# Layer norms behind projections: shift by the mean of the first four tiles, squares of three pairs folded beside the last two projections

## What is computed

```python
def layer_norm_2(x, g, b):
    mu = jnp.mean(xf, -1, keepdims=True)
    var = jnp.mean(jnp.square(xf - mu), -1, keepdims=True)
    return ((xf - mu) * lax.rsqrt(var + LN_EPS_2) * g + b).astype(x.dtype)
...
    h = layer_norm_2(DEEPNORM_ALPHA * h + m, ln_g[i, 0], ln_b[i, 0])
```

## Time and profile before

| | us |
|---|---|
| median of 3 runs | 3078.92 |
| lowest, highest | 3077.69, 3083.2 |
| the profiled execution | 3076.58 |
| its span, first to last instruction | 3074.8 |
| TensorE matmuls busy | 2885.7 (94%) |
| VectorE busy | 858.7 (28%) |
| ScalarE busy | 348.2 (11%) |
| mean granted TensorE clock | 0.994 |

### The profile page before, as it was taken

The page is one execution under the profiler, slowest core; times in us unless marked ns, Lnnn a source line. Parts: engine busy times, 40 slices in busy tenths (PEclk is TensorE's granted clock), DMA queues, the critical chain, the costliest instruction groups (busy, mean ns, idle before and its releaser), DMA issues.

```text
span 3074.8 us, 39592 instructions
## 1 busy us (share of the span) xinstructions
PE 2885.7 (94%) x16504; PEld 2035.2 (66%) x16504; DVE 858.7 (28%) x1787; ACT 348.2 (11%) x710; POOL 52.8 (2%) x92
## 2 busy tenths in 40 slices
PE   6999999998888899999988888999999999999998
PEld 3554444476666667788644444588788887887887
DVE  1332321242222233331311111288522202222201
ACT  0022220020000011220100000101211001011000
POOL 1000000000000001000000000000000000000000
PEclk9999999999999999999999999999999999999999
DMA  8443335169999984234699999943333443342440
GB/s 328 166 156 128 127 119 214 69 243 420 421 417 421 420 349 137 86 102 148 235 421 421 420 420 421 374 147 124 107 123 110 151 151 110 123 144 89 156 144 36
DMA packets 97804, 684.05 MB, mean 222 GB/s; under 512 B 11632, under 2 KB 12784, under 8 KB 17136
## 3 DMA queue, kind: packets, MB, share of 16 engines
q1 hardware_dynamic: 91632, 660.17, 54.3%
q0 software_dynamic: 6016, 21.50, 2.3%
HBM read 678.22 MB, written 3.41 MB: 222 GB/s over the span
## 4 chain that ended last, share of the span: by engine, by line
PE 74%; DMA 22%; DVE 2%; ACT 1%; issue 1%; SPq 0%; ACTq 0%; DVEq 0%
PE ps L612 29%; DMA ring<-units 22%; PE ps L878 11%; PE ps L1044 6%; PE ps L907 3%; PE ps L1348 2%; PE ps L1183 2%; PE ps L630 2%; PE ps L621 1%; PE ps L703 1%; PE ps L699 1%; PE ps L1000 1%; PE ps L928 1%; PE ps L792 1%; PE ps L813 1%; PE ps L1030 1%
## 5 line engine op out<-in xcount | busy, mean ns | idle before, releaser
L612 PE MATMUL ps<-h,ring 128*128 128x256 f32 (+1 forms) x2176 | 501.3, 392 | 4.9 <-ACT h L1507 4.9
L612 PEld LDWEIGHTS ps<-h,ring 128*128 128x128 f32 x2176 | 411.8, 190 | 92.2 <-issue 37.8
L1059 PE MATMUL ps<-ring,arena 128*32 128x256 f32 x3072 | 380.7, 382 | 55.8 <-DMA ring<-units 52.0
L1044 PE MATMUL ps<-ring,arena 128*64 128x256 f32 x3072 | 352.0, 385 | 57.4 <-DMA ring<-units 53.3
L1044 PEld LDWEIGHTS ps<-ring,arena 128*64 128x64 f32 x3072 | 236.5, 138 | 165.7 <-issue 81.9
L1059 PEld LDWEIGHTS ps<-ring,arena 128*32 128x32 f32 x3072 | 184.2, 109 | 244.1 <-DMA ring<-units 102.7
L878 PE MATMUL ps<-u,ring 128*128 128x512 f32 (+1 forms) x1024 | 339.2, 487 | 0.0
L612 PE MATMUL ps<-arena,ring 128*128 128x256 f32 x1408 | 306.6, 379 | 4.7 <-DVE arena L2299 3.4
L612 PEld LDWEIGHTS ps<-arena,ring 128*128 128x128 f32 x1408 | 267.3, 190 | 42.1 <-DVE arena L2299 4.2
L878 PEld LDWEIGHTS ps<-u,ring 128*128 128x128 f32 x1024 | 193.6, 190 | 133.1 <-issue 119.6
L2213 DVE COPY u<-ps 32x512 f32<-32x512 f32 (+1 forms) x128 | 70.9, 554 | 212.4 <-PE ps L1059 119.9
(11 more groups left out here) (330 smaller groups left out, 2592.6 us busy)
## 6 DMA issues: line engine op xcount, KB each, us to landing
ring<-units SPq DMA_DIRECT2D x624, 1024.0 KB, 13.4
arena<-quarters POOLq DMA_DIRECT2D x32, 256.0 KB, 2.9
h<-tokens SPq DMA_DIRECT2D x1, 2048.0 KB, 24.6
arena<-neighbours POOLq DMA_DIRECT2D x32, 64.0 KB, 5.7
arena<-tokens POOLq DMA_DIRECT2D x1, 2048.0 KB, 9.0
arena<-memory POOLq DMA_DIRECT2D x2, 1024.0 KB, 6.3
con<-constants SPq DMA_DIRECT2D x1, 1712.0 KB, 23.1
early_values<-arena POOLq DMA_DIRECT2D x6, 256.0 KB, 5.0
```

The lines of the kernel that those rows point to most:

```text
L612: last = nc.tensor.matmul(ps[:, g + j, 0:n], w[:, kt, j * P:(j + 1) * P], rhs[:, q * KT + kt, 0:n], start=(q == 0 and kt == 0), stop=(q == ...
L1044: last = nc.tensor.matmul(ps[j * slots:(j + 1) * slots, bank, lo:lo + UC], lhsT[:, kt, 0:slots], w[j][:, kt, :], start=(kt == 0), stop=(kt ...
L1059: last = nc.tensor.matmul(ps[j % 4 * slots:(j % 4 + 1) * slots, banks[j // 4], 0:UC], lhsT[:, kt, 0:slots], w[j][:, kt, :], start=(kt == 0 ...
```

## The change

The mean is no longer formed as a whole before squaring. VectorE adds the first two residual pairs to one tile (tiles 0 to 3 folded), and TensorE multiplies this tile with the mean matrix in the middle of the third product (`middle`, `shift_sum`). Twice that value is the shift `off`. VectorE subtracts it from pairs 0 and 1, and for pairs 2 and 3 from the residual operand ahead of the products (`less_shift`). ScalarE squares pairs 0, 1 and 2 as they are ready. VectorE folds tiles 4 and 5 to `rest`, and the six square tiles to one. Behind the fourth product TensorE multiplies `rest`, the folded squares, tiles 6 and 7 and their squares: six matmuls. The variance is the mean square less the square of the rest of the mean, one VectorE instruction, with the square of the rest by ScalarE. VectorE subtracts the rest of the mean from each pair behind that, between the multiplies. In `layer`, `shift_and_values` moves behind the norm's matmuls, and the wait for `memory_loaded` ahead of them.

```diff
...
-            def project(rhs, n, tiles=2, groups=1, arrived=None):
+            def project(rhs, n, tiles=2, groups=1, arrived=None, middle=None):
...
+                        if middle and q == groups // 2 and j == 0:
+                            middle()
...
+            def shift_sum(folded, n, g):
+                pe.wait_ge(part_folded, at(part_folded))
+                nc.tensor.matmul(ps[:, g, 0:n], mean, folded[:, 0, 0:n], start=True, stop=True).then_inc(shift_summed, 1)
+
+            def rest_and_squares(x, sq, rest, n, g):
+
+                pe.wait_ge(rest_folded, at(rest_folded))
+                nc.tensor.matmul(ps[:, g, 0:n], mean, rest[:, 0:n], start=True, stop=False)
+                pe.wait_ge(squares_folded, at(squares_folded))
+                nc.tensor.matmul(ps[:, g + 1, 0:n], mean, sq[:, 0, 0:n], start=True, stop=False)
+                pe.wait_ge(centred, at(centred, KT // 2))
+                for kt in (KT - 2, KT - 1):
+                    last = nc.tensor.matmul(ps[:, g, 0:n], mean, x[:, kt, 0:n], start=False, stop=(kt == KT - 1))
+                last.then_inc(shift_left, 1)
+                pe.wait_ge(squares_ready, at(squares_ready, KT // 2))
+                for kt in (KT - 2, KT - 1):
+                    last = nc.tensor.matmul(ps[:, g + 1, 0:n], mean, sq[:, kt, 0:n], start=False, stop=(kt == KT - 1))
+                last.then_inc(squares_summed, 1)
...
+            def project_and_normalize(rhs, x, sq, n, folded, rest, groups=1, after=None, arrived=None, between=None):
+
+                g = 2 * (state["product"] % 4)
                 for c in range(KT // 2):
-                    project(rhs, n, groups=groups, arrived=None if c else arrived)
-                    if c:
-                        sums(x, n, c - 1, g, *((products_taken, first + c) if taken
-                                               else (residual_ready, at(residual_ready))))
-                sums(x, n, KT // 2 - 1, g, *((products_taken, first + KT // 2) if taken
-                                             else (residual_ready, at(residual_ready))))
+                    project(rhs, n, groups=groups, arrived=None if c else arrived,
+                            middle=(lambda: shift_sum(folded, n, g)) if c == 2 else None)
                 state["product"] += 1
                 count.skip(products_taken, 1)
                 if between:
                     between()
-                squares(sq, n, g)
+                rest_and_squares(x, sq, rest, n, g)
                 if after:
                     after()
...
-                project_and_normalize(merged[l], u, sq1, T, taken=False, between=shift_and_values,
+                project_and_normalize(merged[l], u, sq1, T, gated, gated[:, 1, :], after=shift_and_values,
+                                      between=lambda: pe.wait_ge(memory_loaded, 16 * (l + 1)),
...
+            def shifted_normalize(x, sq, n, tiles, gain, shift, eps):
...
+                act.wait_ge(shift_left, at(shift_left))
+                A(sq[:, KT - 3, 0:n], ps[:, g, 0:n], ACT.Square).then_inc(rest_squared, 1)
+                act.wait_ge(variances_ready, at(variances_ready))
+                link(A(rstd[:, 0:n], rstd[:, 0:n], ACT.Ln, bias=eps))
+                A(rstd[:, 0:n], rstd[:, 0:n], ACT.Exp, scale=-0.5).then_inc(inverses_ready, 1)
...
+            def shifted_normalize(x, sq, n, folded, rest, residual, less_shift, tiles, gain, shift):
+
+                pair = [x[:, 2 * c:2 * c + 2, 0:n] for c in range(4)]
+                off = rstd[:, 0:n]
+                g = 2 * (state["product"] % 4)
+                residual(0)
+                residual(1)
+                settle()
+                link(v.tensor_tensor(folded[:, :, 0:n], pair[0], pair[1], ALU.add))
+                v.tensor_tensor(folded[:, 0, 0:n], folded[:, 0, 0:n], folded[:, 1, 0:n], ALU.add).then_inc(part_folded, 1)
+                dve.wait_ge(shift_summed, at(shift_summed))
+                link(v.tensor_scalar(off, ps[:, g, 0:n], 2.0, None, ALU.mult))
+                for c in range(2):
+                    v.tensor_tensor(pair[c], pair[c], wide(off, [P, 2, n]), ALU.subtract).then_inc(centred, 1)
+                for c in range(2, 4):
+                    less_shift(c, wide(off, [P, 2, n]))
+                settle()
+                residual(2)
+                settle()
+                v.tensor_tensor(rest[:, 0:n], x[:, 4, 0:n], x[:, 5, 0:n], ALU.add).then_inc(rest_folded, 1)
+                for c in range(2):
+                    dve.wait_ge(squares_ready, at(squares_ready, 2 - c))
+                    link(v.tensor_tensor(sq[:, 0:2, 0:n], sq[:, 0:2, 0:n], sq[:, 2 * c + 2:2 * c + 4, 0:n], ALU.add))
+                v.tensor_tensor(sq[:, 0, 0:n], sq[:, 0, 0:n], sq[:, 1, 0:n], ALU.add).then_inc(squares_folded, 1)
+                count.skip(squares_ready, 1)
+                residual(3)
...
+                dve.wait_ge(rest_squared, at(rest_squared))
+                dve.wait_ge(squares_summed, at(squares_summed))
+                v.tensor_tensor(off, ps[:, g + 1, 0:n], sq[:, KT - 3, 0:n], ALU.subtract).then_inc(variances_ready, 1)
+                less_rest(0)
+                less_rest(1).then_inc(dve_step, 1)
+                dve.wait_ge(inverses_ready, at(inverses_ready))
+                dve.wait_ge(dve_step, at(dve_step))
+                scale(0)
+                less_rest(2).then_inc(dve_step, 1)
+                scale(1)
+                less_rest(3).then_inc(dve_step, 1)
+                for c in (2, 3):
+                    dve.wait_ge(dve_step, at(dve_step))
+                    scale(c)
```

More of the change, by code:

```diff
@@ L365, in build @@
         t1, t2 = part(0, KT, S, of=uflat(u)), part(KT * S, KT, S, of=uflat(u))
+        fold, leftover = t2[:, KT - 2:KT, :], small[:, 768:1024]
         mem = h[:, :, S:]
@@ L1350, in out_half @@
                                                     stop=(q == 0 and kt == KT - 1 and j == 1))
+                        if middle and j == 0:
+                            middle()
                     last.then_inc(units_used, 1)
@@ L1836, in normalize, with less_rest, scale @@
                     v.tensor_tensor(pair, pair, wide(rstd[:, 0:n], [P, 2, n]), ALU.mult).then_inc(scaled, 1)
+                state["norm"] += 1
+                taken(mark())
+                dve.wait_ge(scaled, KT // 2 * state["norm"])
+                for kt in range(NORM_ACT, KT):
+                    v.tensor_scalar(tiles[:, kt, 0:n], x[:, kt, 0:n], gain[:, kt:kt + 1], shift[:, kt:kt + 1],
+                                    ALU.mult, ALU.add).then_inc(tail_normed, 1)
+            def shifted_normalize(x, sq, n, folded, rest, residual, less_shift, tiles, gain, shift):
+                pair = [x[:, 2 * c:2 * c + 2, 0:n] for c in range(4)]
+                off = rstd[:, 0:n]
+                g = 2 * (state["product"] % 4)
+                residual(0)
[19 more added lines that the diff above has]
+                residual(3)
+                state["product"] += 1
+                def less_rest(c):
+                    return v.tensor_tensor(pair[c], pair[c], wide(ps[:, g, 0:n], [P, 2, n]), ALU.subtract)
+                def scale(c):
+                    v.tensor_tensor(pair[c], pair[c], wide(off, [P, 2, n]), ALU.mult).then_inc(scaled, 1)
+                dve.wait_ge(rest_squared, at(rest_squared))
[12 more added lines that the diff above has]
+                    scale(c)
@@ L2085, in layer, with residual @@
                     link(v.tensor_scalar(again, again, ALPHA, None, ALU.mult))
-                for c in range(4):
+                def residual(c):
                     g = product()
@@ L2471, in even_mixer, with residual @@
                         .then_inc(conv_ready, 1)
[L2472 removed]
+                def residual(c):
                     dve.wait_ge(units_used, at(units_used))
[L2474 to L2477 removed]
+                    add_product(c, ps[:, outs[c], :].rearrange("p (a n) -> p a n", n=S))
+                latent_norm(0, residual)
             def odd_mixer():
```

98 lines of the change are left out of this document (57 added, 41 removed).

## The result

| | us |
|---|---|
| changed kernel, median of 4 runs | 3041.84 (3040.66 to 3043.0) |
| kernel before, median of 4 runs | 3079.25 (3077.69 to 3083.2) |
| ratio, with its 95% interval | 0.9877 (0.9865 to 0.9889) |
| profiled execution of the changed kernel | 3043.0, span 3041.2 |
| forecast, range | 3039.3, 3033 to 3048 |

The change brings 37.4 us between the medians; the forecast was 39.6.

The account below looks back on a forecast made before the run. The prediction took TensorE as the main bound, with norm matmuls and the elementwise steps between them on the path. Eight norms' gains summed to 41.5 us, less 1.9 for the clock: 39.6, giving 3039.3 us, range 3033 to 3048.

Parts of the forecast that it names:

- The three ahead of zero: Three mean matmuls per norm saved before zero, the end of the last projection product: 1.3 us, 2.6 at 512 columns.
- the two mixers' norms: Norms behind even and odd mixer: six matmuls plus filler, no tile waited for; gain 5.7 us each, 11.4 together.
- The two dates of "ahead of zero": First fold due 3.46 us behind product 1, folded squares due at zero; cover 1.3 and 3.5 us.
- the first cover: Slack of VectorE's fold of four tiles before the shift matmul needs it: 1.3 us.
- The clock term: Longer TensorE rest, 3.2 us, brings the lower clock level behind both memory norms, costing 0.95 us twice, 1.9.
- the hiding of the low level behind the tiles' slow arrival: Behind a memory norm, slowly arriving tiles hide some 0.65 us of the 1.6 a low clock costs.
- The sentence on the odd mixer: The odd mixer's sweep already stood at the low clock level, so its gain stays.
- VectorE's tail: Last steps of each 256-column norm: first multiply starts 4.48 us behind zero, VectorE's two tiles end at 8.96.
- The rival of the tail: VectorE's eight passes don't overlap, 0.72 us each and not 0.60; whole time 3043.3 us; chance 0.14.
- The experts: Rival: expert stage gives the `layer` gains back, 11.8 us lost if transfers aren't tied to TensorE; 3051; chance 0.06.
- The slower rival: TensorE stands at the shift matmul in product 2 if the fold is late; 10 us chain gives 3091; chance 0.03.
- the exposed norms' terms: Gains at full clock: memory norms 4.5 us each, norm from first `mlp` to odd mixer 5.0, last norm 4.3.

Follow-up runs that it names:

- more_mm: Changed kernel plus three further copies of the shift matmul in the middle of the third product in all eight norms; 3056.55 us.
- unfolded: Changed kernel with TensorE summing the six square tiles of the first three pairs behind the last product, instead of VectorE folding them; 3057.21 us.
- late_fold: Changed kernel with the first fold on VectorE done six times instead of once; 3064.93 us.
- second execution: Profiled execution of the changed kernel run again unaltered as a yardstick; that run's time was 3042.32 us.
- second_only: Kernel before with the change in the six norms of the second block alone; 3053.28 us, ratio 0.9910 to the kernel before.
- first_only: Kernel before with the change in the two norms of `layer` alone; 3065.78 us, ratio 0.9946 to the kernel before.
- warm: Changed kernel plus seven filler matmuls on constants behind the norm's matmuls in both memory attentions and both MLPs; 3041.17 us.
- before_warm: Kernel before plus five filler matmuls in the rest behind the squares in both memory attentions and MLPs; one run, 3078.78 us.
- early: Changed kernel with VectorE's subtractions of the rest of the mean reordered, one left between the multiplies; 3043.22 us.

## Why the prediction was right

**The ledger.** The sign, the size (39.6 against 37.4) and the places are those forecast. Nine matmuls of each norm left TensorE's path. The three ahead of zero count in full, by the stretches of the result and by more_mm, and so do matmuls behind it, by unfolded. In the two mixers' norms the terms came out to 0.1 us: filler and six matmuls, no wait for a tile.

**Where TensorE must not wait** it did not. The view of who waited for whom has no wait of a matmul at the shift, `rest`, folded-square or last square matmuls (L648, L653, L655, L662). Their weight loads show 2.5 us of idle time in ten places, all put down to "issue", that is to no other engine. Ahead of tiles 6 and 7 (L658) the weight loads do wait for the last residual add, 1.9 us in six places and 1.4 in two, but the matmuls themselves start only 0.08 late in the second block and 0.2 to 0.3 in the layers. The two dates of "ahead of zero" held. late_fold measured the first cover as 1.36 us. The second can be read in the changed kernel: at the first memory attention's norm the squares are folded at 2321.71, 3.7 us ahead of zero, where 3.5 was forecast.

**The clock term** had the right sign and mechanism. The prediction took 0.95 at each memory norm. Against full clock (14.06, with fillers) it was 1.3 and 1.2, and 1.0 twice in the second execution. The term that was mis-sized is the hiding of the low level behind the tiles' slow arrival: 0.65 was put, and 1.6 less what was found leaves 0.3 to 0.4 (0.6 in the second execution). The sentence on the odd mixer took its low level as a fixture of before and after; it was, in these executions, and the fillers gave back 1.3. This norm gave 3.15 and not 3.7, since its sweep started at 6.08 behind zero and not at 5.94 and took 5.59 us and not 5.21.

**VectorE's tail.** The forecast put the first multiply at 4.48. It came at 4.6 in five norms and at 4.95 in the last. 0.08 of it shows in the variance's start, from the short rests of TensorE (0.18); the rest is in the hand-overs behind it. In the last norm VectorE stood 0.45 us between the second subtraction and the multiply where the other five show 0.1. The trace names only VectorE's own subtraction as what ended it. A second execution shows the same 9.41, the runs second_only and late_fold 9.07. In late_fold the same pause stands in two other norms, behind the first MLP and behind the odd mixer, whose tiles come at 9.43:

```profile
2576.04 0.69 DVE L1916 TENSOR_TENSOR u<-u,small 128x512 f32<-128x512 f32 x1 [0.46 <-DVE u L1913]
```

So it doesn't belong to the last norm, and the cause stays open. In these two kernels the last norm gave 2.5 and not 3.0.

The rival of the tail was wrong in its mechanism: the passes do follow at 0.60, as the timeline shows (0.68 long, 0.60 apart). But the tail does set the end, and the other order took 0.5 to 0.85 off it.

**The experts** gave nothing back; the rival falls by the two stages' lengths, and first_only's whole time lies outside its 0 to 2. **The slower rival** falls by the idle times; late_fold shows what it would have cost had the fold been late.

**What is missing.** The eight norms give 26.1 us behind zero and 11.7 ahead of it: 37.8, against 37.4 and 39.1 between the medians. Of the 2 us by which 39.6 was too much, 1.8 are the exposed norms' terms above. The 33.6 between the two profiled executions is less by stretches with no edit in them. One is the 1.7 us in the first memory attention at low clock. The first norm's zero came 1.6 us earlier and not 2.6, in the second execution even 0.8 later than before, so the time ahead of it varies between executions. Between the norm behind the first experts and layer 1's sweep the gain was 2.4 in the profiled execution and 4.0 in the second one of the same kernel, where 4.0 was expected.

## What to carry to other kernels

Where one engine is busy nearly all the time, take instructions away from it by folding on an engine that is idle, and check when the folded operand must be there, and what is queued behind the wait for it. Where a chain of small steps on several engines is exposed, count what is left on the last engine: two passes per tile pair behind the last statistic can be ordered so that only one lies between the results. And if an edit lengthens a rest of TensorE, look at the granted clock of the stretch behind it; matmuls on constants into a free bank, no longer than the rest, gave back 1.0 to 1.4 us at each norm where the clock had fallen. Count that in whole times, too: in warm and before_warm another stretch was 1.7 us longer instead, and whether the fall had only moved isn't shown.

## What the runs showed of the hardware beyond that

The clock's low level isn't tied to the program alone. The same kernel had it in one execution and not in another behind the same rest (83.97 or 85.65 us for one stage). It isn't by chance alone either. In the six profiled executions that had the change in these norms, the first order on VectorE and no fillers, the clock fell to 0.5 behind all three rests of 3.3 to 3.7 us, 18 times of 18. In early, with another order of some VectorE instructions and rests of 3.38 us, it fell behind one of three; that is one execution, so that the order decides isn't shown. In the kernel before it fell behind one of three rests of 2.46 us. The exposed sweep behind a fall was taken 1.0 to 1.4 us later, and a stage behind one was up to 1.7 longer. In more_mm and late_fold the clock stood low for longer behind the memory norms, and the takes were at 16.2 to 16.4, 2.2 to 2.4 later than 14.06.

Such falls go with the spread of 8 us between runs of one kernel: the runs of the kernel before in the last three sittings with a mean granted clock of 0.995 took 3075.3 to 3078.0 us, those at 0.990 and 0.991 took 3081.8 to 3083.8.
